# A float32 model step on one core: two projections go row tile by row tile, the weights' remainders last

## The chip, the cores and the metric

The kernel runs on one NeuronCore of one Trainium2 chip. The metric is the device time of one execution in microseconds (us). The engines are TensorE (PE), VectorE (DVE), ScalarE (ACT), GpSimd (POOL) and SyncE (SP), which issues most transfers.

## What is computed

For 256 rows (tokens) of width 1024 in float32, two blocks follow each other. The first: an FFT and convolution mixer, cross attention over a memory, and a mixture of 32 experts. The second, which the change touches, in the reference's words:

```
x = rmsnorm(x, norm_final)                         # end of the first block
for layer in range(2):
    shift, scale, gate = ada_modulation(c, ada_w[layer, 0], ada_b[layer, 0])
    h = x * (1.0 + scale) + shift
    y = mixer_ab(h, ...) or mixer_c(h, ...)        # layer 0: h @ ab_w_in (1024 x 1224); layer 1: h @ c_w_in (1024 x 3072)
    x = layer_norm(DN_ALPHA * x + gate * y, ln_g[layer, 0], ln_b[layer, 0])
    shift, scale, gate = ada_modulation(c, ada_w[layer, 1], ada_b[layer, 1])
    h = x * (1.0 + scale) + shift
    x = layer_norm(DN_ALPHA * x + gate * squared_relu_mlp(h, ...), ln_g[layer, 1], ln_b[layer, 1])
```

"Later projections" are those four inputs h of the second block, numbered m0 to m3: m0 goes into `ab_w_in`, m2 into `c_w_in`, m1 and m3 into the MLPs.

## The kernel before

Everything is written out by hand, engine by engine; each engine has one list of instructions, and semaphores tie the lists together. There is no planner: the order in the code is the order on the engine.

Most products are float32 made of three passes. Weights and inputs are split into a main part ("hi", rounded to fp32r) and a remainder ("lo" = value - hi), and `three` (L1192) adds x_hi w_hi, x_hi w_lo and x_lo w_hi into one bank. In the projections the piece of x is the stationary operand (128 x 128), the weights move (408 or 512 columns).

Weights come in granules of 2 MB or less through a ring of slots; SyncE issues a granule's transfer when the slot's former granule has been used up (semaphore `granules_used`, raised by the last matmul on it). ScalarE makes the main part (`split_hi`, L535), VectorE the remainder (`split_lo`, L545; `ab_in_lo`, L2285 to L2292, for the first granule of `ab_in`, in three pieces of 1224 columns). `ab_in` has granules of 3, 3 and 2 chunks of 128 rows; `c_in` six granules of 4 chunks, two for each of its three projections.

How x gets to TensorE: the row tiles (t = 0, 1; 128 rows each) are normalized in `X`; `transpose_hat` (L1697) transposes all 16 blocks of 128 x 128 into banks 4 to 7, a chunk k of both tiles side by side; ScalarE's `evac_hi` (L957, instruction at L967) writes scale * x + shift as main part into `XT_r`, 256 columns at a time, and VectorE's `evac_lo` (L2471, instructions at L2482 and L2487) the remainder into `XTL`. A chunk is usable when both are done (semaphores `xt_a`, `xt_v`).

- m0: behind the last expert, ScalarE splits granule 0 of `ab_in` (its last expert step is written out behind the loop for that), loads the table of the square root, splits granule 1, and squares the rows (L926) once VectorE has added the experts' sum (L2283). VectorE normalizes (L2298, L2299), TensorE transposes behind two filler matmuls (`keep_busy`, L1183), then runs 144 products chunk by chunk: for each chunk both tiles, for each tile three column groups, for each group three passes. At L1849 and after it follow small steps of the attention.
- m2: behind the first MLP, `layer_norm(1)` gives tile 0, then tile 1 (VectorE L2443 and ScalarE L954 write it). TensorE transposes tile 0, runs three filler matmuls, transposes tile 1, then runs `project3` on `c_in`: 96 products for each of the three projections. Between them VectorE makes the remainders of `c_in` 1 to 3, finishes the normalized rows (`affine`) and rotates the first projection's output (`rope`), which the third projection's banks wait for. The split of granules 0 and 1 has been done in the MLP (granule 0's remainder too).

## Time and profile before

| | |
|---|---|
| median of 3 runs | 1861.13 us (1860.92 to 1867.56) |
| profiled execution, its own time | 1863.54 us |
| its span | 1861.7 us |
| PE busy | 1761.7 us (95%) |
| DVE busy | 741.2 us (40%) |
| ACT busy | 533.8 us (29%) |
| share of the chain that ended last | PE 70%, DMA 21%, ACT 4%, DVE 3% |

The durations of the prediction are those of the profiled execution. In the rows, a line "start, length, engine, line, operation, out<-in, form, xN" groups N instructions; the length is that of the whole group, and "idle before <-releaser" tells how long the engine stood and what ended it. ACTq is ScalarE's queue, not its arithmetic. The profile counts a filler matmul (plain float32, 128 x 512) as two instructions.

### The profile page before, as it was taken

What the parts mean: (1) busy time and instruction counts of PE and PEld (TensorE: products, weight loads), DVE (VectorE), ACT (ScalarE), POOL (GpSimd) and SP (SyncE); (2) the same over time, 40 slices, a digit from 0 to 9 for tenths busy, and PEclk for the clock granted to TensorE, in tenths of its full rate; (3) what the DMA queues carried; (4) which work ended last, traced back from release to release, by engine and by line L of the source; (5) the groups of instructions that cost most, each with busy time, mean ns of one, the idle gap of its engine ahead of it and who ended that gap; (6) DMA issues with size and microseconds to landing.
All of it is one profiled execution on the core that took longest, in us unless ns stands there. A gap on an engine that the chain in (4) does not pass through costs nothing.

```text
span 1861.7 us, 24404 instructions
## 1 busy us (share of the span) xinstructions
PE 1761.7 (95%) x9962; PEld 1104.2 (59%) x9962; DVE 741.2 (40%) x1253; ACT 533.8 (29%) x693; POOL 28.2 (2%) x33
## 2 busy tenths in 40 slices
PE   6999999999999999999999999798899999989997
PEld 6787764344444343343434434375699878679986
DVE  3245352122222122121212212368865468675545
ACT  4344430110110110101101010327544453644442
POOL 0101000000000000000000000000000000000001
PEclk9999999999999999999999999998999999999999
DMA  9767899999999999999999999964345555435550
GB/s 340 284 222 279 295 391 428 427 428 427 428 429 429 428 428 428 428 428 429 429 429 428 428 428 429 372 214 169 116 172 189 196 189 187 175 114 181 180 203 24
DMA packets 96703, 587.68 MB, mean 316 GB/s; under 512 B 7118, under 2 KB 7332, under 8 KB 71044
## 3 DMA queue, kind: packets, MB, share of 16 engines
q1 hardware_dynamic: 95348, 582.12, 77.4%
q10 hardware_dynamic: 1296, 4.72, 0.7%
q8 instruction: 44, 0.72, 0.2%
q14 instruction: 15, 0.12, 0.0%
HBM read 585.77 MB, written 1.05 MB: 315 GB/s over the span
## 4 chain that ended last, share of the span: by engine, by line
PE 70%; DMA 21%; ACT 4%; DVE 3%; issue 1%; SPq 0%; ACTq 0%; DVEq 0%
PE bank L1192 34%; DMA ring<-in_w_gate_up 20%; PE bank L1486 14%; PE bank L1505 8%; PE bank L1433 4%; PE bank L1516 1%; PE bank L1281 1%; PE bank L1266 1%; PE bank L1478 1%; ACT arena L906 1%; PE bank L1498 1%; PE bank L1667 1%; ACT w_hi L535 1%; PE bank L1849 0%; PE bank L1654 0%
## 5 line engine op out<-in xcount | busy, mean ns | idle before, releaser
L1486 PE MATMUL bank<-ring,arena 128*64 128x512 f32 x2048 | 463.3, 597 | 31.4 <-DMA ring<-in_w_gate_up 31.4
L1486 PEld LDWEIGHTS bank<-ring,arena 128*64 128x64 f32 x2048 | 137.3, 136 | 323.5 <-issue 253.9
L1192 PE MATMUL bank<-w_hi,arena_r 128*128 128x512 f32 (+1 forms) x784 | 257.8, 391 | 4.7 <-DVE arena_r L2333 2.8
L1505 PE MATMUL bank<-ring,arena 128*64 128x512 f32 x1024 | 226.8, 595 | 3.3
L545 DVE TENSOR_TENSOR w_lo<-ring,w_hi 128x4096 fp32r<-128x4096 f32 (+2 forms) x43 | 188.1, 4375 | 53.0 <-ACT w_hi L535 50.8
L535 ACT ACTIVATE w_hi<-ring 128x4096 fp32r<-128x4096 f32 (+2 forms) x45 | 159.0, 3573 | 45.4 <-DMA ring<-in_c_w_out 25.4
L904 ACT ACTIVATE arena<-arena,sb_tab 128x512 f32<-128x512 f32 x32 | 23.1, 722 | 511.8 <-DVE arena L2188 511.8
L2188 DVE TENSOR_SCALAR arena<-bank 128x512 f32<-128x512 f32 x32 | 22.1, 692 | 370.7 <-PE bank L1486 370.7
L1192 PEld LDWEIGHTS bank<-w_hi,arena_r 128*128 128x128 f32 x784 | 148.1, 189 | 35.5 <-DVE arena_r L2333 3.3
L1505 PEld LDWEIGHTS bank<-ring,arena 128*64 128x64 f32 x1024 | 71.7, 137 | 137.8 <-issue 132.2
L1192 PE MATMUL bank<-XT_r,w_hi 128*128 128x256 f32 x512 | 146.5, 286 | 4.4 <-DVE arena_r L2487 4.4
L1192 PE MATMUL bank<-arena_r,w_hi 128*128 128x256 f32 x512 | 145.5, 284 | 0.0
L1192 PE MATMUL bank<-XT_r,w_lo 128*128 128x256 f32 x512 | 145.4, 284 | 0.0
L1433 PEld LDWEIGHTS bank<-arena,sb_XN 128*128 128x128 f32 x1056 | 123.2, 192 | 26.0 <-issue 26.0
L1433 PE MATMUL bank<-arena,sb_XN 128*128 128x64 f32 x1056 | 128.4, 275 | 0.0
L1192 PE MATMUL bank<-w_lo,arena_r 128*128 128x512 f32 x320 | 124.9, 390 | 0.0
L2209 DVE SCALAR_TENSOR_TENSOR arena_r<-bank,sb_att,arena_r 128x512 fp32r<-128x512 f32 x32 | 24.0, 750 | 217.4 <-ACT arena_r L909 217.4
L1192 PEld LDWEIGHTS bank<-XT_r,w_hi 128*128 128x128 f32 x512 | 98.9, 193 | 5.8 <-issue 5.3
L1192 PEld LDWEIGHTS bank<-arena_r,w_hi 128*128 128x128 f32 x512 | 98.9, 193 | 1.0 <-issue 0.5
L1192 PEld LDWEIGHTS bank<-XT_r,w_lo 128*128 128x128 f32 x512 | 98.8, 193 | 0.0
L909 ACT ACTIVATE arena_r<-bank,sb_att 128x512 fp32r<-128x512 f32 x32 | 22.0, 688 | 231.1 <-PE bank L1505 231.1
L522 DVE TENSOR_TENSOR half_lo<-ring,half_hi 128x2048 fp32r<-128x2048 f32 x24 | 55.0, 2291 | 81.2 <-ACT half_hi L512 81.1
(389 smaller groups left out, 2103.1 us busy)
## 6 DMA issues: line engine op xcount, KB each, us to landing
ring<-in_w_gate_up SPq DMA_DIRECT2D x128, 2048.0 KB, 32.0
ring<-in_w_down SPq DMA_DIRECT2D x64, 2048.0 KB, 35.3
ring<-in_mlp_w SPq DMA_DIRECT2D x32, 2048.0 KB, 8.3
ring<-in_ada_w SPq DMA_DIRECT2D x22, 2048.0 KB, 12.0
ring<-in_c_w_in SPq DMA_DIRECT2D x6, 2048.0 KB, 7.7
ring<-in_w_in SPq DMA_DIRECT2D x4, 2048.0 KB, 9.8
ring<-in_w_k SPq DMA_DIRECT2D x2, 2048.0 KB, 12.4
ring<-in_w_v SPq DMA_DIRECT2D x2, 2048.0 KB, 8.5
```

Source lines behind the costliest of these rows:

```text
L522: eng.tensor_tensor(lo[:], half_raw(name, h)[1], hi[:].bitcast(F32), ALU.subtract).then_inc(sem("w_lo"), 1)
L535: act.activation(pair(g)[0][:, 0:w], slot(slot_of(g), w), ACT.Copy).then_inc(sem("w_hi"), 1)
L545: eng.tensor_tensor(lo[:, 0:w], slot(slot_of(granule_no(name, i)), w), hi[:, 0:w].bitcast(F32), ALU.subtract).then_inc(sem("w_lo"), 1)
L904: act.activation(sig, gcl, ACT.Sigmoid, bias=zero, scale=1.702).then_inc(sem("e_sig"), 1)
L906: act.activation(hT, B[0][:].rearrange("p (c n) -> p c n", c=4), ACT.Copy).then_inc(sem("e_hTe"), 1)
L909: act.activation(y_hi, B[2][:], ACT.Copy, scale=slot_gate).then_inc(sem("e_y"), 1)
L1192: mm = pe.matmul(out, st[a], mv[b], start=start and a + b == 0, stop=stop and a == 1, skip_group_check=True)
L1433: mm = pe.matmul(B[3][:, k * CAP:(k + 1) * CAP], XN[:, t, k * P:(k + 1) * P], sel_tok[:, t, :], start=(t == 0), stop=(t == 1))
L1486: mm = pe.matmul(B[m][CAP * h:CAP * h + CAP, :], xe[:, 2 * j + kl, :], w[:, kl, m * D + h * HW:m * D + (h + 1) * HW], start=False, stop=(j ...
L1505: mm = pe.matmul(B[2][CAP * h:CAP * h + CAP, :], hT[:, c, CAP * j:CAP * j + CAP], w[:, c, h * HW:(h + 1) * HW], start=(j == 0 and c == 0), ...
L2188: dve.tensor_scalar(gcl, B[0][:], 7.0, None, ALU.min).then_inc(sem("e_clamp"), 1)
L2209: dve.scalar_tensor_tensor(y_lo, B[2][:], slot_gate, y_hi.bitcast(F32), ALU.mult, ALU.subtract).then_inc(sem("e_ylo"), 1)
```

## The change

1. ScalarE's last expert step goes back into the loop. The first two thirds of granule 0 of `ab_in` are split before the squares, the last third after the second root; granule 1 is split between the evacuations of the two tiles, no longer ahead of the squares.
2. VectorE makes the first two pieces of the remainder behind tile 0's and tile 1's normalization, the third behind the second.
3. For m0 and m2 the transposes go tile by tile: tile t uses banks 4 + 2t and 5 + 2t, 128 columns a block, and both engines evacuate 128 columns at a time (twice as many instructions of half the size). For m2 the first four blocks of tile 0 are evacuated before tile 1's root.
4. TensorE no longer runs `three` there but a written order of steps (granule, tile, x part, w part): main parts first, the weights' remainder last in each granule, and products of tile 0 ahead of the transposes of tile 1. Filler: five matmuls instead of two at m0, none instead of three at m2.

```diff
-            def expert(i, down_done, ahead=None):
+            def expert(i, down_done):
...
-                if ahead is not None:
-                    split_hi(act, *ahead)
-
-            with act.Fori(0, NE - 1) as i:
+
+            with act.Fori(0, NE) as i:
                 expert(i, (used, i * PER_E + (NPRE + PER_E)))
-            expert(NE - 1, (used, MOE_END), ("ab_in", 0))
...
             act.activation(stat[:, 59:60], eps5, ACT.Sqrt, bias=zero)
-            split_hi(act, "ab_in", 1)
+            ab_in_hi(0, 2)
...
+            def evac_tile(a, t, ks):
+
+                g1, g0 = modcol(a)
+                act.wait_ge(sem("mod_g"), 4)
+                for k in ks:
+                    if k % 4 == 0:
+                        act.wait_ge(*upto(f"m{a}", "T", 2 * t + k // 4 + 1))
+                    act.activation(XT_r[:, k, t * P:(t + 1) * P], B[4 + 2 * t + k // 4][:, k % 4 * P:k % 4 * P + P],
+                                   ACT.Identity, scale=g1(k), bias=g0(k)).then_inc(sem("xt_a"), 1)
...
-            evac_hi(0)
+            ab_in_hi(2, 3)
+            evac_tile(0, 0, range(KC))
+            split_hi(act, "ab_in", 1)
+            evac_tile(0, 1, range(KC))
             split_hi(act, "ab_in", 2)
...
             ln_hat(1, 0)
+            evac_tile(2, 0, range(4))
             ln_root(1, 1)
             ln_hat(1, 1)
-
-            evac_hi(2)
+            evac_tile(2, 0, range(4, KC))
+            evac_tile(2, 1, range(KC))
...
+            def project_tiles(a, grans, outs, width, order, ready):
+
+                for step in order:
+                    if step == "T":
+                        transpose_tile(a, 1)
+                        continue
+                    if step == "banks":
+                        pe.wait_ge(*upto(f"m{a}", "xt_v", KC))
+                        continue
+                    n, t, xa, wa, last = step
+                    parts, ks = grans[n]
+                    for kl, k in enumerate(ks):
+                        pe.wait_ge(*upto(f"m{a}", ("xt_a", "xt_v")[xa], KC * t + k + 1))
+                        ready(n, wa, kl)
+                        x = (XT_r, XTL[a])[xa]
+                        for c, b in enumerate(outs[t]):
+                            mm = pe.matmul(b, x[:, k, t * P:(t + 1) * P], parts[wa][:, kl, width * c:width * c + width],
+                                           start=k + xa + wa == 0, stop=False, skip_group_check=True)
+                    if last:
+                        mm.then_inc(used, 1)
...
-            keep_busy(0, 2)
-            transpose_hat(0)
...
+            keep_busy(0, 5)
+            transpose_tile(0, 0)
...
+                          [(0, 0, 0, 0, False), "T", (0, 0, 0, 1, False), (0, 0, 1, 0, False), (1, 0, 0, 0, False), "banks",
+                           (0, 1, 0, 0, False), (0, 1, 0, 1, False), (1, 1, 0, 0, False), (0, 1, 1, 0, True),
+                           (1, 0, 1, 0, False), (1, 1, 1, 0, False), (1, 0, 0, 1, False), (1, 1, 0, 1, True),
+                           (2, 0, 0, 0, False), (2, 1, 0, 0, False), (2, 0, 1, 0, False), (2, 1, 1, 0, False),
+                           (2, 0, 0, 1, False), (2, 1, 0, 1, True)], ab_in_ready)
...
-            transpose_hat(2)
+            transpose_tile(2, 0)
             x2 = (XT_r, XTL[2])
-            project3(x2, 0, ready=2)
...
+                          [(0, 0, 0, 0, False), (0, 0, 0, 1, False), "T", (0, 0, 1, 0, False), (0, 1, 0, 0, False),
+                           (0, 1, 0, 1, False), (1, 0, 0, 0, False), (1, 1, 0, 0, False), (0, 1, 1, 0, True),
+                           (1, 0, 1, 0, False), (1, 1, 1, 0, False), (1, 0, 0, 1, False), (1, 1, 0, 1, True)], c_in_ready)
...
-            ab_in_lo(0)
             for t in range(TB):
                 dve.wait_ge(*upto("fin", "root", t + 1))
                 link(dve.reciprocal(stat[:, 80 + t:81 + t], stat[:, 18 + t:19 + t]))
                 dve.tensor_scalar(X[:, t, :], X[:, t, :], stat[:, 80 + t:81 + t], None, ALU.mult).then_inc(
                     sem("xhat"), 1)
-            ab_in_lo(1)
+                ab_in_lo(dve, t)
+            ab_in_lo(dve, 2)
```

How the lists move, at the places of the prediction. TensorE at m0, behind the experts, before:

```order
L1183 MATMUL bank<-sb_tab 128x512 x2
L1710 MATMUL bank<-sb_tab,sb_X 128x128 [waits xhat]
L1710 MATMUL bank<-sb_tab,sb_X 128x128 x7
L1710 MATMUL bank<-sb_tab,sb_X 128x128 [waits xhat]
L1710 MATMUL bank<-sb_tab,sb_X 128x128 x7
L1192 MATMUL bank<-w_hi_49,XT_r 128x408 [waits xt_v,xt_a,ab_in_part]
L1192 MATMUL bank<-w_lo_50,XT_r 128x408
L1192 MATMUL bank<-w_hi_49,arena_r 128x408
```

and now (XT_r is x's main part, arena_r its remainder):

```order
L1217 MATMUL bank<-sb_tab 128x512 x5
L1763 MATMUL bank<-sb_tab,sb_X 128x128 [waits xhat]
L1763 MATMUL bank<-sb_tab,sb_X 128x128 x7
L1783 MATMUL bank<-w_hi_49,XT_r 128x408 [waits ab_in_hi,xt_a]
L1783 MATMUL bank<-w_hi_49,XT_r 128x408 x2
L1783 MATMUL bank<-w_hi_49,XT_r 128x408 [waits ab_in_hi,xt_a]
L1783 MATMUL bank<-w_hi_49,XT_r 128x408 x2
L1783 MATMUL bank<-w_hi_49,XT_r 128x408 [waits w_hi,xt_a]
L1783 MATMUL bank<-w_hi_49,XT_r 128x408 x2
L1763 MATMUL bank<-sb_tab,sb_X 128x128 [waits xhat]
L1763 MATMUL bank<-sb_tab,sb_X 128x128 x7
L1783 MATMUL bank<-w_lo_50,XT_r 128x408 [waits ab_in_part,xt_a]
```

Nine products of tile 0 have moved ahead of tile 1's transposes, and each run of three has its own two waits.

ScalarE at the same place, from the end of the experts on, now:

```order
L933 ACT_TABLE_LOAD
L933 ACTIVATE sb_stat<-sb_tab 128x1
L940 ACTIVATE w_hi_49<-ring 128x2448 [waits slot7_landed]
L946 ACTIVATE sb_XN,sb_stat<-sb_X,sb_tab 128x1024 [waits moe_x]
L949 ACTIVATE sb_stat<-sb_stat,sb_tab 128x1 [waits sq]
L946 ACTIVATE sb_XN,sb_stat<-sb_X,sb_tab 128x1024 [waits moe_x]
L949 ACTIVATE sb_stat<-sb_stat,sb_tab 128x1 [waits sq]
L940 ACTIVATE w_hi_49<-ring 128x1224 [waits slot7_landed]
L997 ACTIVATE XT_r<-bank,sb_mod 128x128 [waits T,mod_g]
```

Before the squares stand 2448 columns of split, where two splits of 3672 stood.

TensorE at m2, behind the first MLP, now (before: eight transposes, three fillers, eight transposes, then the products of `three`):

```order
L1763 MATMUL bank<-sb_tab,sb_X 128x128 [waits xhat_a]
L1763 MATMUL bank<-sb_tab,sb_X 128x128 x7
L1783 MATMUL bank<-w_hi_51,XT_r 128x512 [waits w_hi,xt_a]
L1783 MATMUL bank<-w_hi_51,XT_r 128x512
...
L1783 MATMUL bank<-w_lo_52,XT_r 128x512 [waits w_lo,xt_a]
L1783 MATMUL bank<-w_lo_52,XT_r 128x512
L1763 MATMUL bank<-sb_tab,sb_X 128x128 [waits xhat]
L1763 MATMUL bank<-sb_tab,sb_X 128x128 x3
L1763 MATMUL bank<-sb_tab,sb_X 128x128 [waits xhat_a]
L1763 MATMUL bank<-sb_tab,sb_X 128x128 x3
L1783 MATMUL bank<-w_hi_51,arena_r 128x512 [waits w_hi,xt_v]
```

Sixteen products of tile 0 stand where the fillers stood.

## Rows read from the trace of the kernel before

**Rows 1.** The page: granted clock in 40 slices, and the chain that ended last, by line.

```profile
PEclk9999999999999999999999999998999999999999
...
PE bank L1192 34%; DMA ring<-in_w_gate_up 20%; PE bank L1486 14%; PE bank L1505 8%; PE bank L1433 4%; PE bank L1516 1%; PE bank L1281 1%; PE bank L1266 1%; PE bank L1478 1%; ACT arena L906 1%; PE bank L1498 1%; PE bank L1667 1%; ACT w_hi L5
```

**Rows 2.** The chain in order of time, first place: start us, us, what.

```profile
1210.29 28.56 PE bank L1192 x144
1238.88 1.57 DVE arena L2545 x3
```

**Rows 3.** The same view, second place.

```profile
1534.47 56.30 PE bank L1192 x240
1590.79 7.64 DMA ring<-in_c_w_out
```

**Rows 4.** Windows: us, busy of each engine, PEclk (granted clock), DMA share, GB/s.

```profile
1204.00:1206.00 2.00, 0.67 (x3) 0.67 (x4) 1.10 (x4) 1.72 (x4) 0.00 (x0) 0.50 1.05 386
...
1535.00:1538.00 3.00, 3.00 (x8) 2.33 (x8) 2.93 (x9) 3.00 (x3) 0.00 (x0) 0.50 0.00 0
```

**Rows 5.** Timeline, ScalarE, first place: start us, us, engine line op, idle before.

```profile
1194.82 3.26 ACT L535 ACTIVATE w_hi<-ring 128x3672 fp32r<-128x3672 f32 x1
1198.09 1.28 ACT L922 ACT_TABLE_LOAD   x1
...
1199.59 3.25 ACT L535 ACTIVATE w_hi<-ring 128x3672 fp32r<-128x3672 f32 x1
1202.74 1.13 ACT L926 ACTIVATE sb_XN<-sb_X,sb_tab 128x1024 f32<-128x1024 f32 x1
...
1207.82 3.76 ACT L967 ACTIVATE XT_r<-bank,sb_mod 128x256 fp32r<-128x256 f32 x8 [2.07 <-PE bank L1710]
1211.43 2.28 ACT L535 ACTIVATE w_hi<-ring 128x2448 fp32r<-128x2448 f32 x1
```

**Rows 6.** The chain in order of time, ScalarE's queue (ACTq) in the first place.

```profile
1194.34 0.48 ACTq L917
...
1195.34 0.02 ACTq L531
```

**Rows 7.** Timeline, VectorE, first place.

```profile
1197.30 2.48 DVE L2283 TENSOR_TENSOR sb_X<-bank,sb_X 128x512 f32<-128x512 f32 x4 [1.59 <-PE bank L1516]
...
1206.65 1.43 DVE L2292 TENSOR_TENSOR w_lo<-ring,w_hi 128x1224 fp32r<-128x1224 f32 x1
```

**Rows 8.** Timeline, TensorE, first place; the last two are consecutive.

```profile
1205.33 3.67 PE L1710 MATMUL bank<-sb_tab,sb_X 128*128 128x128 f32 x16 [6.21 <-DVE sb_X L2299]
...
1217.59 0.35 PE L1192 MATMUL bank<-w_hi,XT_r 128*128 128x408 f32 x1
1217.77 0.34 PE L1192 MATMUL bank<-w_lo,XT_r 128*128 128x408 f32 x1
```

**Rows 9.** Timeline, TensorE, second place.

```profile
1527.61 1.03 PE L1710 MATMUL bank<-sb_tab,sb_X 128*128 128x128 f32 x8
1528.48 2.74 PE L1183 MATMUL bank<-sb_tab 128*128 128x512 f32 x6
1531.48 1.09 PE L1710 MATMUL bank<-sb_tab,sb_X 128*128 128x128 f32 x8 [0.26 <-DVE sb_X L2443]
...
1535.19 0.63 PE L1192 MATMUL bank<-w_hi,arena_r 128*128 128x512 f32 x1
1535.62 0.63 PE L1192 MATMUL bank<-w_hi,XT_r 128*128 128x512 f32 x1
```

**Rows 10.** Timeline, VectorE, second place.

```profile
1530.88 0.54 DVE L2443 TENSOR_SCALAR sb_X<-sb_X,sb_att 128x512 f32<-128x512 f32 x1
1533.06 0.88 DVE L2482 SCALAR_TENSOR_TENSOR sb_XN<-bank,sb_mod,XT_r 128x256 f32<-128x256 f32 x2 [1.64 <-ACT XT_r L967]
1533.97 0.62 DVE L2487 TENSOR_SCALAR arena_r<-sb_XN,sb_mod 128x256 fp32r<-128x256 f32 x2
...
1538.94 13.49 DVE L545 TENSOR_TENSOR w_lo<-ring,w_hi 128x4096 fp32r<-128x4096 f32 x3
```

More of the change, by code:

```diff
@@ L204 @@
     SHARES[_kind] = [(st, 4) for st in TURNS]
-SHARES["xt_a"] = [(st, 4 if st == "ffn" else 8) for st in TURNS]
+SHARES["xt_a"] = [(st, {"ffn": 4, "m0": 16, "m2": 16}.get(st, 8)) for st in TURNS]
 SHARES["xt_v"] = SHARES["xt_a"]
@@ L546, in split_lo, with ab_in_lo @@
                               ALU.subtract).then_inc(sem("w_lo"), 1)
+        def ab_in_lo(eng, k):
+            g = granule_no("ab_in", k // 3)
+            n, cut = split_no(g), slice(k % 3 * 1224, (k % 3 + 1) * 1224)
+            hi, lo = pair(g)
+            if k < 2:
+                eng.wait_ge(sem("ab_in_hi"), 1)
+            else:
+                eng.wait_ge(sem("w_hi"), n)
+            eng.wait_ge(sem("w_lo"), n - 1)
+            ins = eng.tensor_tensor(lo[:, cut], slot(slot_of(g))[:, cut], hi[:, cut].bitcast(F32), ALU.subtract)
+            ins.then_inc(*((sem("w_lo"), 1) if k % 3 == 2 else (sem("ab_in_part"), 1)))
         @block.sync
@@ L922, in _, with ab_in_hi @@
             act.activation(stat[:, 59:60], eps5, ACT.Sqrt, bias=zero)
-            split_hi(act, "ab_in", 1)
+            def ab_in_hi(a, b):
+                g = granule_no("ab_in", 0)
+                cut = slice(a * 1224, b * 1224)
+                act.wait_ge(landed[slot_of(g)], FILL[g])
+                act.activation(pair(g)[0][:, cut], slot(slot_of(g))[:, cut], ACT.Copy).then_inc(
+                    *((sem("w_hi"), 1) if b == 3 else (sem("ab_in_hi"), 1)))
+            ab_in_hi(0, 2)
             for t in range(TB):
@@ L1715, in transpose_hat, with transpose_tile @@
                         keep_busy(0, 3)
+            def transpose_tile(a, t):
+                st = "fin" if a == 0 else f"ln{a - 1}"
+                if a == 0:
+                    pe.wait_ge(*upto(st, "xhat", t + 1))
+                elif t == 0:
+                    pe.wait_ge(*upto(st, "xhat_a", 1))
+                else:
+                    pe.wait_ge(*upto(st, "xhat", 1))
+                for k in range(KC):
+                    if a and t == 1 and k == 4:
+                        pe.wait_ge(*upto(st, "xhat_a", 2))
+                    mm = pe.transpose(B[4 + 2 * t + k // 4][:, k % 4 * P:k % 4 * P + P], X[:, t, k * P:(k + 1) * P], ident)
+                    if k % 4 == 3:
+                        mm.then_inc(sem("T"), 1)
+            def project_tiles(a, grans, outs, width, order, ready):
[17 more added lines that the diff above has]
+                        mm.then_inc(used, 1)
             def x_chunk(a, k):
@@ L1915, in _, with c_in_ready @@
             mlp(0)
-            transpose_hat(2)
+            transpose_tile(2, 0)
             x2 = (XT_r, XTL[2])
-            project3(x2, 0, ready=2)
+            g2 = at[0]
+            at[0] += 2
+            def c_in_ready(n, wa, kl):
+                pe.wait_ge(sem(("w_hi", "w_lo")[wa]), split_no(g2 + n))
+            project_tiles(2, [(chunks(pair(g2 + j), 4), range(4 * j, 4 * j + 4)) for j in range(2)],
+                          [[B[2 * t + h][:] for h in range(2)] for t in range(TB)], HW,
+                          [(0, 0, 0, 0, False), (0, 0, 0, 1, False), "T", (0, 0, 1, 0, False), (0, 1, 0, 0, False),
+                           (0, 1, 0, 1, False), (1, 0, 0, 0, False), (1, 1, 0, 0, False), (0, 1, 1, 0, True),
+                           (1, 0, 1, 0, False), (1, 1, 1, 0, False), (1, 0, 0, 1, False), (1, 1, 0, 1, True)], c_in_ready)
             project3(x2, 4)
@@ L2469, in affine_ready, with evac_tile @@
                     dve.wait_ge(*upto(f"ln{a - 1}", "ln_landed", 32))
+            def evac_tile(a, t):
+                g1, g0 = modcol(a)
+                for q in range(2):
+                    dve.wait_ge(*upto(f"m{a}", "xt_a", KC * t + 4 * q + 4))
+                    for k in range(4 * q, 4 * q + 4):
+                        if t:
+                            dve.wait_ge(*upto(f"m{a}", "xt_v", k + 1))
+                        ins = dve.scalar_tensor_tensor(XN[:, 0, k * P:(k + 1) * P], B[4 + 2 * t + q][:, k % 4 * P:k % 4 * P + P],
+                                                       g1(k), XT_r[:, k, t * P:(t + 1) * P].bitcast(F32), ALU.mult,
+                                                       ALU.subtract)
+                    link(ins)
+                    for k in range(4 * q, 4 * q + 4):
+                        dve.tensor_scalar(XTL[a][:, k, t * P:(t + 1) * P], XN[:, 0, k * P:(k + 1) * P], g0(k), None,
+                                          ALU.add).then_inc(sem("xt_v"), 1)
             def evac_lo(a):
@@ L2474, in evac_lo @@
                 for q in range(4):
-                    if a == 0 and q == 1:
-                        ab_in_lo(2)
                     dve.wait_ge(*upto(f"m{a}", "xt_a", 2 * q + 2))
@@ L2520, in mlp @@
                 mlp_group(l, 3, True, ahead)
-            evac_lo(0)
+            for t in range(TB):
+                evac_tile(0, t)
             split_lo(dve, "ab_in", 1)
@@ L2627, in _ @@
             layer_norm(1, "mlp0", 15)
-            evac_lo(2)
+            for t in range(TB):
+                evac_tile(2, t)
             for i in range(1, 4):
```

40 lines of the change are left out of this document (10 added, 30 removed).

## The prediction

> **What bounds the kernel now.** I read four views in this order. First the chain that ended last, by line [rows 1]: TensorE's matmuls of the split products (L1192) hold 34% of the span and the experts' weights most of the rest, so TensorE is the bound outside the expert loop. Then the same chain in order of time around the two places that the change touches. In the first place (after the last expert) 144 matmuls of `ab_in` run from 1210.29 for 28.56 us, and at 1238.88 the copies of the result start [rows 2]; the transposes ahead of them start at 1205.33 [rows 8]. In the second place (behind the first MLP) 240 matmuls of `c_in` start at 1534.47, and a transfer follows them [rows 3]. All of what stands ahead of 1210.29 and 1534.47 is exposed. Third the windows: the granted clock is 0.50 (the 1.2 GHz level) in 1204 to 1206 and again in 1535 to 1538 [rows 4], behind 6.21 us and 1.9 us in which TensorE stood idle [rows 8, 9]. Last the timelines of the three engines in the two places [rows 5 to 10], for durations.
>
> **The change, stage one.** ScalarE today splits a whole granule after its last expert step (3.26 us), loads a table (1.28), splits a second granule (3.25), and squares the first rows only at 1202.74 [rows 5]. The change leaves two thirds of one split there. ScalarE's queue got past the skipped overflow block at 1195.34 [rows 6], so I put the table load at 1195.5; plus 1.28, plus 0.2 for the one-element root (what lies between the table load and the split at 1199.59), plus 2.28 (the row of 2448 columns) gives the square at 1199.3, 3.4 us sooner. VectorE's adds of both row tiles start at 1197.30 and take 2.48 for four [rows 7], so the first tile is there. Everything that hangs on the square moves by 3.4: the transposes from 1205.33 to 1201.9.
>
> The Trainium skill's page "Runtime: NRT & Kernel Launch", section "Instruction fetch mechanics", speaks against this move: a taken branch that leaves the prefetched pages must first fetch its target. The same skip in the trace cost no more than 1.0 us from the read of the count (1194.34) to the next wait (1195.34) [rows 6], then hidden behind the 3.26 us split. By the trace the stage gains what is worked out here; by the rule it would begin later by one fetch, which no row prices, and this is part of rival two.
>
> TensorE's filler grows from 2 to 5 matmuls. The profile counts each as two; six of these took 2.74 us [rows 9], with the tail about 0.43 each, so ten end near 1201.6, ahead of the transposes. TensorE is then idle for some 1.3 us in pieces, not the 6.21 us of before [rows 8], and I take the clock to stay at 2.4 GHz.
>
> ScalarE next makes the last third (1.1), from 1202.3 to 1203.4, then eight 128-column evacuations. Eight of 256 columns took 3.76 [rows 5]; the slope between the two split rows (3.25 and 2.28 us for 3672 and 2448 columns) is 0.8 ns a column, so one of 128 costs about 0.36. That is 16 x 0.36 = 5.8 in place of 3.8 us, beside TensorE's work. The first product starts at 1203.9. A product costs 0.185 us at full clock [rows 8]. Nine (1.7) reach 1205.6, the second tile's transposes (its rows ready at 1204.2) 1206.5. The nine with the weights' remainder need VectorE: norm of tile 0 ends 1201.9, a third of the remainder 1.43 [rows 7] 1203.3, norm of tile 1 1204.2, two more thirds 1207.0. So these end at 1208.2. The nine with x's remainder need VectorE's first small pieces. From the 256-column pairs (0.88 and 0.62 for two [rows 10]; the second duration is that of the same operation in the first stage) less 128 elements I take 0.3 and 0.2; four and one, with the link between, reach 1208.6. **This is the one wait I expect.** From there 144 - 18 = 126 products x 0.185 = 23.3 end at 1231.9. Against 1238.7 (1210.29 + 28.56, less about 0.15 for the tail of the last record) that is **-6.8 us**.
>
> Later needs, with their slack: granule 1 main part 1209.5 (needed 1210.2); banks of tile 0 read by VectorE 1211.2 (needed 1211.9); remainder of granule 1 1219.3, that is four quarters of 2.0 us and at most three thirds of 1.43 [rows 7] behind 1207.0 (needed 1221.9); of granule 2 about 1224.6 (needed 1229.7). The bounds of the 128-column pieces, which today's kernel does not have: if halving saves nothing (VectorE 0.44 and 0.31, ScalarE 0.47), the bank wait costs 1.1 us, the remainder of granule 1 another 0.3, and in stage two the remainder of c_in 2 comes 1.2 us late; if it halves the cost, only the wait at 1208 goes (0.4). I take the values by the slope, which are nearest to the rows, and keep +2.6 and -0.4 for the range.
>
> **Stage two.** Today the transposes of tile 0 start at 1527.61, three filler matmuls follow, tile 1's transposes take 1.09 from 1531.48 after a wait of 0.26 [rows 9], and the first product waits 1.9 us more, with the first nine at 0.43 in place of 0.227 us ((56.30 - 9 x 0.43) / 231 = 0.227 [rows 3, 9]). The change fills the gap: evacuation of four chunks of tile 0 from 1528.2, sixteen products of granule c_in 0 (main part and remainder were made in the MLP) from 1528.7. 16 x 0.227 = 3.6 gives 1532.3; I take 1532.0, since the last product's tail overlaps what follows. The transposes' inputs are there by then: VectorE's part by 1531.42 [rows 10], and the same transposes ran through from 1531.48 [rows 9]. They reach 1533.0. x's remainder for tile 0: VectorE free at 1531.4, first chunk at about 1532.9. Then 80 x 0.227 = 18.2 end at 1551.2. Before: 1534.47 + 9 x 0.43 + 87 x 0.227 = 1558.1. That is **-6.9 us**; if the sixteen really end at 1532.3, -6.6.
>
> What is late next: VectorE's evacuation takes 4 x 2.0 = 8.0 in place of 5.9 us but starts at 1531.4, not 1533.06; its three weight remainders (13.49 [rows 10]) then start near 1539.3, and hand over at 1543.8, 1548.3 and 1552.8, needed at 1547.5, 1551.2 and 1562. After them come two affine steps and the rotations of the first 1024 columns, ready near 1566, needed by the third projection at 1573. The output projection's second granule is fetched when c_in 4 is used up, a TensorE event, so the 7.64 us transfer in the chain [rows 3] moves with it. Removing the three filler matmuls is free: the products stand in their place.
>
> Granules go back to the fill queue later in the order (the first after 72 products, not 54, and after 64, not 48) but not later in time: 1218.5 where it is about 1222 today, and 1543.9 where it is about 1547, so SyncE's queue, which waits for nothing else there, sends each transfer sooner.
>
> The same holds between the stages: no transfer ends a wait in the chain from 1210 to 1590 but that one, so stage one's gain arrives at the end. The peeled last expert step going back into ScalarE's loop costs nothing by itself; it only removes code.
>
> **Sum.** -6.8 - 6.9 = -13.7 us, of which about 0.4 us is in doubt by the sixteen. The profiled execution (span 1861.7, itself 1863.54) becomes 1849.8; the median of the three runs, 1861.13, becomes 1847.4. I say 1847.5. A measurement of this kernel tells about 0.5%, or 9.3 us, from no change: faster means under 1851.8.
>
> **Rivals.** *One, the clock sinks anyway.* For: in both places an idle stretch was followed by 0.50 [rows 4], and some idle pieces stay in stage one. Against: they are 1.3 us together, and stage two has almost none. Price: nine products at 0.43 in place of 0.227 cost 1.8 us; once or twice gives 1849.3 to 1851.1, still faster. The page "TensorE: Matmul & The Clock Gate", section "HAM oscillation — how this bites in real kernels", says that work behind a long enough wait starts cold. By that rule, which the rows around 1204 bear out, fewer waits keep it warm.
>
> *Two, only one stage pays.* Stage one rests on ScalarE starting at once after a loop exit, a load and a branch, and on two slacks of 0.7 us; stage two on VectorE's queue. If either stage gives nothing, -6.8: 1854.3, within 0.5%. Against: no row shows such a delay.
>
> *Three, slower.* Products now take x and weights in runs of three (stage one) or two (stage two), and each run has two waits of its own: 144/3 + 96/2 = 96 pairs, where it was one pair per 18 or 12. If every pair stopped TensorE as a wait that really ends late does (0.26 us idle before the transposes at 1531.48 [rows 9]), 96 x 0.26 = 25.0 us would turn -13.7 into +11.3: 1872.4. It breaks even at 0.14 us a pair. Against: in `c_in` today two waits per twelve products show no gap within 56.30 us [rows 3], so a wait that is already met costs nothing at that density. At 0.05 to 0.14 us a pair this is part of the "no change" case.
>
> **Numbers.** Forecast 0.67; clock 0.13; one stage or half-paid waits 0.16; slower 0.04. Faster: 0.67 + 0.13 = 0.80; same 0.16; slower 0.04. The range reaches down to 1844, since the span has one more slice whose mean clock is 8 tenths [rows 1], and a low stretch there may shorten when the work behind stage one comes sooner (3 us, an estimate from that digit), and up to 1855, past the one-stage case.
>
> **What would show it.** The profile after should have the transposes near 1202, `ab_in` done by 1232, one short wait for VectorE at 1208, clock 1.00 through 1202 to 1214 and (6.8 earlier than today's times) through 1525 to 1531, and `c_in`'s first projection over 13.7 us sooner. Wrong would be: 128-column evacuations over 0.45 us, gaps between runs of three products, a table load on ScalarE later than 1196, or VectorE's remainder of granule 1 after TensorE wants it.

## The result, and the profile after

The changed kernel takes **1850.97 us** (median of 6 executions, 1844.03 to 1851.34), the kernel before 1862.63 (median of 6). The ratio is 0.9924, 95% interval [0.9904, 0.9944]. The profiled execution took 1850.79 us with a span of 1849.0, where the one before had 1861.7: -12.7 us.

The page of the changed kernel, busy line and the slices of the granted clock:

```profile
PE 1759.2 (95%) x9962; PEld 1103.7 (60%) x9962; DVE 744.7 (40%) x1285; ACT 539.0 (29%) x711; POOL 28.1 (2%) x33
...
PEclk9999999999999999999999999998999999999999
```

The clock's line is digit for digit that of [rows 1]. Its slices of 46 us are too coarse for what follows: low stretches have moved between the two kernels, and only windows show it.

**Stage one.** The chain in order of time (start us, us, what):

```profile
1201.44 1.94 PE bank L1783 x9
1203.38 0.87 PE bank L1763 x8
1204.25 25.13 PE bank L1783 x135
1229.38 0.02 issue
1229.41 1.57 DVE arena L2627 x3
```

The copies of the result start at 1229.41 where they started at 1238.88 [rows 2], 9.47 us sooner. But not all of this is the change's. The timeline of TensorE of the kernel before has the last product of the expert loop at

```profile
1195.85 1.19 PE L1516 MATMUL bank<-arena_r 64*128 64x512 f32 x8 [1.73 <-DVE arena_r L2209]
```

and that of the changed kernel, from the same product on,

```profile
1193.82 1.19 PE L1550 MATMUL bank<-arena_r 64*128 64x512 f32 x8 [1.67 <-DVE arena_r L2286]
1195.14 4.56 PE L1217 MATMUL bank<-sb_tab 128*128 128x512 f32 x10
1199.53 1.07 PE L1763 MATMUL bank<-sb_tab,sb_X 128*128 128x128 f32 x8
1201.44 1.94 PE L1783 MATMUL bank<-w_hi,XT_r 128*128 128x408 f32 x9 [0.84 <-ACT XT_r L997]
1203.22 1.03 PE L1763 MATMUL bank<-sb_tab,sb_X 128*128 128x128 f32 x8
1204.01 1.90 PE L1783 MATMUL bank<-w_lo,XT_r 128*128 128x408 f32 x9
1205.76 1.93 PE L1783 MATMUL bank<-w_hi,arena_r 128*128 128x408 f32 x9
```

The expert loop, which the change leaves to the weights' transfers, ended 2.03 us sooner in this execution. From that product to the copies it is 43.03 us before and 35.59 after: **-7.44 us**. The first product starts 7.62 us behind the expert product (1201.44), where it started 14.44 us behind it (1210.29 [rows 2]). The idle time ahead of it explains most of that: 0.84 us now, in place of 6.21 us ahead of the transposes [rows 8] and 1.29 us more behind them. The remainder products at 1205.76 have no idle time in brackets: the wait for VectorE that I expected there is absent.

The engines that feed them, ScalarE and then VectorE, timelines:

```profile
1193.29 1.28 ACT L933 ACT_TABLE_LOAD   x1 [0.40 <-issue]
1194.58 0.29 ACT L933 ACTIVATE sb_stat<-sb_tab 128x1 f32<-128x1 f32 x1
1194.78 2.23 ACT L940 ACTIVATE w_hi<-ring 128x2448 fp32r<-128x2448 f32 x1
1196.92 1.13 ACT L946 ACTIVATE sb_XN<-sb_X,sb_tab 128x1024 f32<-128x1024 f32 x1
...
1200.95 2.87 ACT L997 ACTIVATE XT_r<-bank,sb_mod 128x128 fp32r<-128x128 f32 x8
```

```profile
1204.26 1.12 DVE L2546 SCALAR_TENSOR_TENSOR sb_XN<-bank,sb_mod,XT_r 128x128 f32<-128x128 f32 x4
1205.42 0.88 DVE L2551 TENSOR_SCALAR arena_r<-sb_XN,sb_mod 128x128 fp32r<-128x128 f32 x4
```

The square starts 3.10 us behind the expert product (6.89 before, [rows 5]). Eight pieces of 128 columns take ScalarE 2.87 us, 0.36 each; four take VectorE 1.12 and 0.88. A quarter (four and four) takes 1.95 us, from 1204.26 to the next at 1206.21.

**Stage two.** The chain, then rows of TensorE's timeline:

```profile
1522.58 3.96 PE bank L1783 x16
1526.53 0.87 PE bank L1763 x8
1527.41 18.16 PE bank L1783 x80
```

```profile
1521.37 1.03 PE L1763 MATMUL bank<-sb_tab,sb_X 128*128 128x128 f32 x8
1522.58 2.13 PE L1783 MATMUL bank<-w_hi,XT_r 128*128 128x512 f32 x8 [0.17 <-ACT XT_r L997]
...
1545.41 0.39 PE L1226 MATMUL bank<-w_hi,XT_r 128*128 128x512 f32 x1
```

The transposes of tile 0 start at 1521.37 (1527.61 before, [rows 9]); sixteen products fill the gap, and the next projection starts at 1545.41. That is 24.04 us behind the transposes. Before, it was 30.35 us (the 97th of the 240 products of [rows 3] starts at 1557.96): -6.3 us.

**The clock, and what went back.** Windows of the changed kernel (columns: us, busy of PE, PEld, DVE, ACT, POOL, then the granted clock as a share of 2.4 GHz, DMA share, GB/s):

```profile
1194.00:1232.00 38.00, 37.03 (x206) 31.45 (x209) 29.70 (x64) 21.96 (x38) 0.00 (x0) 1.00 0.64 232
1238.00:1242.00 4.00, 4.00 (x6) 1.50 (x5) 3.27 (x16) 0.00 (x0) 0.00 (x0) 0.58 1.06 389
1262.00:1273.00 11.00, 9.31 (x38) 5.41 (x38) 10.31 (x41) 10.50 (x25) 0.00 (x0) 0.53 0.00 1
1283.00:1290.00 7.00, 7.00 (x36) 3.37 (x35) 4.29 (x17) 3.05 (x11) 0.00 (x0) 0.51 0.12 23
1337.00:1341.00 4.00, 3.53 (x17) 3.56 (x18) 3.92 (x12) 1.50 (x4) 0.00 (x0) 0.57 0.14 57
1516.00:1550.00 34.00, 33.83 (x158) 27.95 (x157) 32.16 (x55) 19.11 (x23) 0.00 (x0) 1.00 0.45 158
```

Both stages run at 1.00 throughout; in both the kernel before had 0.50 windows [rows 4]. So part of both gains is the clock. In stage two the kernel before had nine products at 0.43 in place of 0.227 us, 1.8 us. In stage one its products stood 0.34 us apart at first, in place of 0.185:

```profile
1211.11 0.54 PE L1192 MATMUL bank<-w_hi,arena_r 128*128 128x408 f32 x1
1211.45 0.54 PE L1192 MATMUL bank<-w_hi,XT_r 128*128 128x408 f32 x1
```

The low stretch ended at 1213.9, some ten products in, which makes about 1.6 us, an estimate from these two distances; its transposes were slow too.

Between the stages TensorE sits at 1.2 GHz for 23.8 us, summed over windows of 1 us, and the kernel before only for 17.0 (23.9 and 17.1 by the clock's own records). The way from the copies of stage one to the transposes of stage two grew from 288.73 to 291.96 us: 3.2 us of stage one's gain went back there. The experiments had to tell whether the change does that.

I cut each execution at five marks: E, the expert product above; Z, the copies; M, the first product behind the first attention; T, the transposes of stage two; Y, the first product behind the second attention. In brackets: us at 1.2 GHz in the stretch (behind Y the low stretch at the program's end, which every kernel has, is left out).

| kernel | E to Z | Z to M | M to T | T to Y | Y to end |
|---|---|---|---|---|---|
| before | 43.03 (10.2) | 74.96 (17.0) | 213.77 (0) | 109.82 (3.4) | 224.27 (3.4) |
| changed | 35.59 (0) | 76.71 (20.4) | 215.25 (3.4) | 103.38 (0) | 224.25 (3.4) |
| changed, again | 35.60 (0) | 73.06 (13.6) | 213.77 (0) | 103.52 (0) | 224.38 (3.4) |
| s1_only | 35.60 (0) | 75.03 (17.0) | 215.26 (3.4) | 109.78 (3.4) | 224.41 (3.4) |
| s2_only | 43.07 (10.2) | 74.98 (17.0) | 213.79 (0) | 104.81 (3.4) | 224.43 (3.4) |
| t_first | 35.71 (0) | 76.56 (20.4) | 215.29 (3.4) | 108.94 (6.8) | 224.51 (3.4) |
| fill2 | 36.16 (3.4) | 71.63 (10.2) | 215.15 (3.4) | 104.80 (3.4) | 224.49 (3.4) |
| split_back | 40.49 (3.4) | 73.09 (13.6) | 213.74 (0) | 103.63 (0) | 224.32 (3.4) |
| lo_early | 38.90 (3.4) | 71.55 (10.2) | 215.07 (3.4) | 106.25 (3.4) | 224.27 (3.4) |
| warm_mlp | 35.58 (0) | 73.36 (13.6) | 213.75 (0) | 103.43 (0) | 223.01 (0) |
| warm_mlp, again | 35.60 (0) | 73.57 (13.6) | 213.75 (0) | 104.88 (3.4) | 222.98 (0) |
| warm_ix | 35.57 (0) | 77.15 (13.6) | 215.08 (3.4) | 104.84 (3.4) | 224.44 (3.4) |
| warm_all | 37.06 (3.4) | 79.40 (20.4) | 213.74 (0) | 106.60 (6.8) | 222.96 (0) |

### The profile page after: what moved, and what is told of

Same layout as the page of the kernel before. It is cut to its first block, busy times and chain, and to the rows that moved or that the text cites. A ratio compares the mean times of both kernels' runs of the same rounds, so it can differ in the third digit from the quotient of the medians.

```text
span 1849.0 us, 24540 instructions
## 1 busy us (share of the span) xinstructions
PE 1759.2 (95%) x9962; PEld 1103.7 (60%) x9962; DVE 744.7 (40%) x1285; ACT 539.0 (29%) x711; POOL 28.1 (2%) x33
## 4 chain that ended last, share of the span: by engine, by line
PE 73%; DMA 20%; ACT 4%; DVE 3%; issue 1%; SPq 0%; ACTq 0%; DVEq 0%
PE bank L1226 32%; DMA ring<-in_w_gate_up 19%; PE bank L1520 15%; PE bank L1539 8%; PE bank L1467 4%; PE bank L1783 3%; PE bank L1550 1%; PE bank L1315 1%; PE bank L1300 1%; PE bank L1512 1%; ACT arena L920 1%; PE bank L1532 1%; PE bank L1701 1%; PE bank L1688 0%; PE bank L1916 0%
## 5 line engine op out<-in xcount | busy, mean ns | idle before, releaser
L1226 PE MATMUL bank<-w_hi,arena_r 128*128 128x512 f32 x704 | 227.5, 392 | 4.7 <-DVE arena_r L2400 2.8
L1226 PEld LDWEIGHTS bank<-w_hi,arena_r 128*128 128x128 f32 x704 | 132.3, 188 | 33.9 <-DVE arena_r L2400 3.3
```

The lines of the kernel that those rows point to most:

```text
L1226: mm = pe.matmul(out, st[a], mv[b], start=start and a + b == 0, stop=stop and a == 1, skip_group_check=True)
```

## The experiments

**One stage each.** s1_only keeps the first stage and restores the third projection; s2_only the reverse.

```diff
-            transpose_tile(2, 0)
...
+            transpose_hat(2)
+            x2 = (XT_r, XTL[2])
+            project3(x2, 0, ready=2)
```

> The first stage as changed, the third projection as it was before. My theory: the stages gain by themselves, and what lies between gives some back by the granted clock. The first stage's consumers should come 7.4 us sooner than before (and the two or so more that the expert loop may take less by itself), the way from the second attention's transposes to the first output 63.9 us as before (1527.6 to 1591), and the whole 1854 to 1858 us. Rival, only one stage pays and it is the second: 1861 to 1863. Rival, the clock's low stretches move with every shift of a few us: then the sum is off from 1862.6 - 7.4 - 2 by one or two times 1.7 us, and the windows show another count of low stretches between the stages.

> The third projection as changed, the first stage as it was. My theory: the stretches up to 1527 us of the span read as before, the way from the first transposes of that stage to the first output load shrinks by 6.3 us, and the whole is 1855.5 to 1857 us; the low stretches of the clock ahead of the stage lie where they lay before (1248, 1272 to 1282, 1292, 1535 us). Rival, only the first stage pays: 1862 to 1863. Where the two single runs together take off 3 us more than the changed kernel did, the 3 us are given back only when the two shifts meet.

s1_only: 1856.85 us (median of 10), ratio 0.9964 [0.995, 0.9978]. s2_only: 1856.73 (10), 0.9978 [0.9962, 0.9995]. By the table the stages' gains are independent: 35.60 and 109.78 us in the one, 43.07 and 104.81 in the other. Rival two, that only one stage pays, is out for the first stage as for the second. Both medians lie in the ranges that I expected. Against the kernel before in the same series (1862.76) they are 5.9 and 6.0 us lower, 11.9 together, and the changed kernel was 11.7 lower in its own series, so the totals show no loss that comes only when both changes meet. My expectation for s2_only erred in its detail: a new low stretch at 1625 cost 1.4 us, and its executions spread from 1854.4 to 1863.84.

**The transposes first.** Tile 1's transposes ahead of all products, in both places.

```diff
-                          [(0, 0, 0, 0, False), "T", (0, 0, 0, 1, False), (0, 0, 1, 0, False), (1, 0, 0, 0, False), "banks",
+                          ["T", (0, 0, 0, 0, False), (0, 0, 0, 1, False), (0, 0, 1, 0, False), (1, 0, 0, 0, False), "banks",
...
-                          [(0, 0, 0, 0, False), (0, 0, 0, 1, False), "T", (0, 0, 1, 0, False), (0, 1, 0, 0, False),
+                          ["T", (0, 0, 0, 0, False), (0, 0, 0, 1, False), (0, 0, 1, 0, False), (0, 1, 0, 0, False),
```

> The changed kernel with tile 1's transposes ahead of every product in both places. My theory: in the first stage nothing of weight (tile 1's rows are there before tile 0's first evacuated piece, so the transposes fill that wait): 0 to +0.4 us; in the third projection TensorE stands until the second tile's normalised rows come and the sixteen products of tile 0 no longer lie in that wait: +3.6 to +4.0 us; together 1854.5 to 1855.5 us. Rival, the products in that wait only displace products that would have waited for VectorE's evacuation anyway: 0 to +1 us, 1851 to 1852. Second rival: the idle engine lets the clock sink, +1.8 us more, up to 1857.

1856.62 us (7), 0.9963 [0.9951, 0.9974], above the 1854.5 to 1855.5 of my theory and within the second rival's reach. Stage one 35.71: +0.1. Stage two, TensorE's timeline:

```profile
1522.05 1.03 PE L1763 MATMUL bank<-sb_tab,sb_X 128*128 128x128 f32 x8
1525.92 1.97 PE L1763 MATMUL bank<-sb_tab,sb_X 128*128 128x128 f32 x8 [2.83 <-DVE sb_X L2510]
1527.54 2.87 PE L1783 MATMUL bank<-w_hi,XT_r 128*128 128x512 f32 x8
```

2.83 us idle, then transposes that take 1.97 in place of 1.03 and eight products 2.87 in place of 2.13: the clock has sunk. From the transposes to the next projection it is 28.17 us (1550.22) against 24.04: +4.1. About 1.7 us of this are the clock (0.94 in the transposes, 0.74 in the products); the rest is the idle time that the sixteen products had filled. So these products are worth 4.1 of stage two's 6.3 us, partly because they keep the engine at work and the clock up, and next to nothing of stage one's gain comes from the products ahead of the second transposes.

**The place of the squares.** split_back puts granule 0's last third and granule 1's split back ahead of the squares.

```diff
             ab_in_hi(0, 2)
+            ab_in_hi(2, 3)
+            split_hi(act, "ab_in", 1)
             for t in range(TB):
...
-            ab_in_hi(2, 3)
             evac_tile(0, 0, range(KC))
-            split_hi(act, "ab_in", 1)
```

> The changed kernel with the third piece of granule 0 and all of granule 1 split by ScalarE ahead of the squares again (the split of granule 1 was there before the change). My theory: the first product of the stage hangs on the squares, so it comes later by these two instructions, 1.1 + 3.2 = 4.3 us, and nothing behind takes it back, because TensorE works without a wait from its first product on: from the last expert's product to the copies of the projection's result 35.6 us become 39.5 to 40.0, and 1 us more where the idle engine's clock falls: 1855 to 1856.5 us. Rival, the order of the products made the gain and the squares' place did not: 35.6 to 37 us, 1851 to 1852.5.

TensorE then reads

```profile
1201.78 1.09 PE L1763 MATMUL bank<-sb_tab,sb_X 128*128 128x128 f32 x8 [4.08 <-DVE sb_X L2365]
1203.05 3.36 PE L1783 MATMUL bank<-w_hi,XT_r 128*128 128x408 f32 x9 [0.17 <-ACT XT_r L999]
```

The stage takes 40.49 us, +4.9. The transposes start 4.24 us later behind the expert product (9.95 against 5.71 us), as two instructions more in the queue should give. The first product starts 3.60 us later (11.22 against 7.62), because granule 0's last third no longer stands between transposes and evacuation. The nine products then take 3.36 us, not 1.94: 1.4 us for the clock, which fell behind 4.08 us idle. All but 0.1 reaches the copies. **Putting this order of ScalarE's queue back costs 4.9 us, two thirds of stage one's 7.4: 3.6 by the wait, the rest by the clock that the wait let fall.** The other third is not taken apart to the end: the half-size evacuations were not tested alone. The whole took 1850.94 us (median of 4, 1848.93 to 1856.71), ratio 0.9951 [0.9934, 0.9967], not the 1855 to 1856.5 that I expected. The changed kernel in the same series had 0.9939 [0.992, 0.9958], so the totals do not show the 4.9 us. The profiled execution had no low stretch between M and Y, as the changed kernel's second had none. The spread over so few executions (8 and 13 us) is larger than the effect; only the marks, of one profile, resolve it.

**The weights' remainder products early.** lo_early puts them right behind the main ones of their granule and tile:

```diff
...
-                           (0, 1, 0, 0, False), (0, 1, 0, 1, False), (1, 1, 0, 0, False), (0, 1, 1, 0, True),
-                           (1, 0, 1, 0, False), (1, 1, 1, 0, False), (1, 0, 0, 1, False), (1, 1, 0, 1, True),
+                           (0, 1, 0, 0, False), (0, 1, 0, 1, False), (0, 1, 1, 0, True),
+                           (1, 0, 0, 0, False), (1, 0, 0, 1, False), (1, 0, 1, 0, False),
...
```

> The changed kernel with the weights' remainder products right behind the main ones of their granule and tile in both places instead of last; tiles stay apart. My theory: in the first stage granule 1's remainder, which VectorE finished at about 1216.3 us of the span, is wanted by TensorE at about 1214, so 2 to 2.5 us of waiting come in: from the last expert's product to the copies of the projection's result 35.6 us become 37.6 to 38.1; in the third projection the remainders are there in time and the stage keeps its length (103.4 us, or 104.8 with a low stretch of the clock near 1620); the whole 1852 to 1854 us plus or minus the clock. Rival, putting these products last buys nothing: 35.6 us stay.

```profile
1193.25 6.25 PE L1217 MATMUL bank<-sb_tab 128*128 128x512 f32 x10
...
1215.57 1.91 PE L1783 MATMUL bank<-w_lo,XT_r 128*128 128x408 f32 x9 [2.09 <-DVE w_lo L545]
...
1533.57 2.08 PE L1783 MATMUL bank<-w_lo,XT_r 128*128 128x512 f32 x8 [0.99 <-DVE w_lo L545]
```

2.09 us of waiting, as expected, so "last" is worth 2 us in stage one. I missed two things. One is a wait of 0.99 in stage two, where T to Y takes 106.25, 1.4 more than 104.85 with the same low stretch. The other is the clock: five fillers took 6.25 us at the low level and held up the transposes, so that the first product came 1.0 us later (8.59 against 7.62), which brings stage one to +3.3. 1853.43 us (6), 0.9957 [0.9943, 0.997].

**The fillers of stage one.** fill2: two fillers instead of five (`keep_busy(0, 2)`).

> The changed kernel with two filler rounds instead of five ahead of the first stage's transposes. My theory, rival one of the prediction: TensorE then stands for about 2.7 us before the transposes, the granted clock may go to its lower level there, and one low stretch of 3.4 us at half rate costs 1.7 us, which shows as a window below 0.8 within 1199 to 1210: 1852.6 us. Other outcome: the gap is too short to matter, the clock stays at 1.00, 1850.8 to 1851.2 us, and the fillers that are needed were two. Nothing of the output depends on the fillers.

```profile
1196.15 1.98 PE L1217 MATMUL bank<-sb_tab 128*128 128x512 f32 x4
1200.56 1.97 PE L1763 MATMUL bank<-sb_tab,sb_X 128*128 128x128 f32 x8 [2.42 <-DVE sb_X L2365]
1202.49 2.61 PE L1783 MATMUL bank<-w_hi,XT_r 128*128 128x408 f32 x9
```

The clock fell, behind 2.42 us idle, but stage one lost 0.6 us, not 1.7. The slow transposes only used up the 0.84 us that TensorE stood before: the first product starts 7.62 us behind the expert product here too (1202.49), and only the nine products (2.61 in place of 1.94) add time. The whole was 1849.75 us (4), ratio 0.9936 [0.9914, 0.9958], lower than the 1850.97 of the changed kernel; in the profiled execution only 10.2 us were slow between Z and M. That says nothing for the two fillers. A total of these kernels also depends on how much low clock an execution happens to have.

**Fillers elsewhere.** warm_ix fills the 2.85 us idle in which the low stretch at 1262 begins; warm_mlp fills the 2.17 us ahead of the MLPs' first products; warm_all is both with fill2.

```diff
+            pe.wait_ge(sem("ix_relu"), 5)
+            keep_busy(6, 3)
             pe.wait_ge(sem("ix_relu"), 8)
...
                             pe.wait_ge(*upto(st, "xhat_a", 2))
+                        if a and t == 1 and k == 6:
+                            keep_busy(0, 2)
```

> The changed kernel with three rounds of filler matmuls in the 2.85 us in which TensorE stands before the third pair of scores of the first attention (1260.8 to 1263.7 us); nothing of the output depends on them. My theory: the six profiles so far have from the copies of the first projection's result to the transposes of the third projection 279.9 us plus half of the time that the granted clock was at its lower level (10.2 to 23.8 us of it), so the idle times there are paid through the clock. If this gap causes the 10.2 us low stretch at 1262.5, the way falls from 292.0 us to about 286.9; if the stretch only moves behind the next gaps, to 288.5 to 290.5; rival, the low stretch comes from something else: 292.0, or more by what the fillers delay. The whole 1845.8 us, 1848 to 1849, or 1851.

> The changed kernel with two rounds of filler matmuls inside the second tile's transposes of the two other projections (the hidden layers' inputs), where TensorE stands 2.17 us ahead of its first product; nothing of the output depends on them. My theory: the low stretches at 1337 and 1655 us of the changed kernel's profile (3.4 us each) go: 1.7 us less for each, 1847.5 us in all; at worst they delay the last evacuated piece by 0.2 us a place. Rival, the low stretches there come from the sparse work before, and stay: 1851.0 to 1851.4.

> The two kinds of filler together, and two rounds instead of five ahead of the first stage (0.6 us longer there in its profile, by a low stretch at 1200). My theory: the gains add as far as the low stretches go: 1843 to 1846 us. Rival, the low stretches only wander with any shift, so that this is one more throw between 1846 and 1854 us.

warm_ix: 1853.14 us (8), 0.9952 [0.9937, 0.9967], no gain. In the kernels without this filler Z to M follows one line: 71.6, 73.1 to 73.6, 75.0, 76.6 us for 10.2, 13.6, 17.0, 20.4 us slow. warm_ix has 13.6 and takes 77.15. Its timeline of TensorE:

```profile
1267.27 1.92 PE L1701 MATMUL bank<-ring,sb_cs 128*32 128x512 f32 x16
1272.19 0.87 PE L1688 MATMUL bank<-sb_tab,sb_XN 128*128 128x128 f32 x6 [3.00 <-DVE sb_XN L2452]
```

The stretch went from 1262, and TensorE then stood 3.00 us for VectorE's top-k and softmax. The six products at 1272.19 start 41.70 us behind Z, against 42.50 and 42.23 in the changed kernel's two profiles: the slow stretch taken away gave back 0.8 us at most. So the slow time there had mostly been hidden by VectorE; the new low stretch, at 1273 to 1281, lies where TensorE bounds. The line was a property of one pattern, and my theory that any filled gap pays is wrong. warm_all (1850.51 us, 5 executions, 0.9939 [0.9922, 0.9956]) missed its 1843 to 1846 us and shows the same: 79.40.

warm_mlp: 1846.46 us (4), 0.9912 [0.9889, 0.9936]; windows at its two places, to be read against 0.57 at 1337 above:

```profile
1337.00:1341.00 4.00, 3.55 (x24) 2.75 (x23) 3.81 (x11) 2.79 (x7) 0.00 (x0) 1.00 0.51 207
...
1655.00:1659.00 4.00, 3.52 (x29) 3.56 (x30) 3.92 (x12) 1.43 (x4) 0.00 (x0) 1.00 0.13 51
```

**Side by side.** The changed kernel and warm_mlp again, on one chip:

> The changed kernel as it is, for a comparison on one chip. Both theories: 1850 to 1852 us, the stage 35.6 us, the third projection's way 103.4 us or 104.8.

> The changed kernel with two filler rounds inside the second tile's transposes of the two hidden layers' inputs, again, beside the changed kernel. My theory: 2.5 to 4 us below it in the median (two low stretches of the clock at 1.3 to 1.7 us each), 1847 to 1848.5 us, with the first products of both places at 0.12 us a pair from the start. Rival, the 4.5 us between the medians so far were the luck of four runs: 1850 to 1852 us.

1849.02 us (6 executions, 1844.38 to 1856.94; ratio 0.9939 [0.992, 0.9958]) against 1848.09 (6, 1843.23 to 1851.22; 0.992 [0.9906, 0.9934]). The difference of 0.9 us is not the 2.5 to 4 that I expected, and the intervals overlap, so the total doesn't prove the fillers. The table does more: Y to end is 223.0 in all three kernels with them and 224.25 to 224.51 in the ten without, and M to T has no low stretch in three of three, where it had one in six of ten. That is -1.4 us in the second place, and -1.4 in the first whenever the clock would have sunk. Over all executions of both series, which ran on different chips, the medians are 1850.8 (12) and 1848.1 (10), 2.7 apart. It has the lowest median of all versions that I ran.

The changed kernel's second profile bears on the 3.2 us. Same program, other execution:

```profile
1261.00:1272.00 11.00, 8.41 (x35) 4.69 (x36) 10.23 (x39) 10.18 (x23) 0.00 (x0) 0.53 0.00 1
1283.00:1290.00 7.00, 6.90 (x63) 4.12 (x62) 6.49 (x29) 5.56 (x22) 0.34 (x2) 1.00 0.54 177
1333.00:1337.00 4.00, 3.12 (x26) 3.15 (x27) 3.89 (x13) 1.92 (x5) 0.00 (x0) 1.00 0.26 104
```

No low stretch at 1283 and none at the first MLP. Z to T takes 286.83 us, less than before the change, and the span is 1844.2. So the change does not have to give anything back. Whether it makes the give-back more likely is not shown. The two profiles with the old stage one have 288.73 and 288.77 us from Z to T; the nine with the new one and without filler between Z and M have 286.6 to 287.3 six times and 290.3 to 292.0 three times.

## Why the prediction was right, and where its steps were off

The total, 1847.5, was 3.5 us low; the range and the side were right (the ratio's interval ends at 0.9944, below the 0.995 that I had asked for). Of the 3.5 us, 1.5 are the starting point: I took the 1861.13 us of three executions, and the median of six is 1862.63. The other 2.0 are the gain, 11.7 us between the medians for the forecast 13.7. By its steps:

- **ScalarE ahead of the squares, -3.4**: right in kind, 0.4 short. Behind the expert product the square came 3.8 us sooner (6.89 to 3.10). The table load behind the loop's exit and the skipped block was there 0.2 us sooner than I put it, with 0.40 us idle ahead of it. The Trainium skill's page "Runtime: NRT & Kernel Launch" (section "Instruction fetch mechanics") says that a taken branch out of the prefetched pages must fetch its target first; the trace shows no wait longer than these 0.40 us. split_back gives the step from the other side: 3.6 us at the first product and 4.9 with the clock.
- **128-column pieces, 0.36 on ScalarE, 2.0 us a quarter on VectorE**: right (0.36; 1.95). The slope between two sizes of the same operation was a better guide here than halving or not halving.
- **"This is the one wait I expect", 0.4 us at 1208**: wrong, no wait. Counted from the expert product the first product came 0.4 us sooner than I had it, and VectorE's first pieces were there at 1205.7, where TensorE came for them at 1205.76. It cost the sum nothing, since the 126 products behind took 23.65 us, not 23.3.
- **Stage one, -6.8**: measured -7.44, three times over (35.59, 35.60, 35.60). Of the 0.6 missing, 0.4 is that earlier first product, the rest my reading of the old end as 1238.7, where [rows 2] has 1238.88. The absent wait (0.4) and the slower 126 products (0.35) cancel. With 1.6 us or more of low clock in the old stage, this step names the queue but not how much of its gain is the clock.
- **Stage two, -6.9, or -6.6 if the sixteen end late**: they did. In the chain they take 3.96 us, not the 3.6 by which even the late value went; the first eight, which follow ScalarE's pieces, need 1.96 us from start to start, not 1.82. To the next projection it gave -6.3, and T to Y -6.44 in the profile and -6.3 in the second. So this term was 0.3 to 0.6 us too large.
- **"No transfer ends a wait between the stages, so stage one's gain arrives at the end"**: true of transfers, but the step left out the clock. There are 13 to 24 us at 1.2 GHz between the stages in every profile, and the changed kernel's two differ by 10.2 us. In the first the way between them took 3.2 us back; in the second it took nothing. This is the step that failed: `c_in`'s second projection starts 12.55 us sooner (1545.41 against 1557.96) where over 13.7 was forecast, and that with the 2.03 us of the expert loop. The profile's account is -7.44 - 6.44 + 3.23 - 2.03 (expert loop) = -12.68, for -12.7 measured. The two stages together gave 13.9 us, a little more than the sum of the forecast; that this execution's total came near (12.7 for 13.7) is luck in part, the 2.0 us of the expert loop, which no step of the forecast moved. Behind the expert product the program is 10.7 us shorter in the first profile and 15.6 in the second. I had let the clock vary only by a slice at the front.
- **Rivals.** Rival one, the clock sinking anyway, did not come in the two stages of the changed kernel, but did elsewhere at about its price (1.4 us each, for 1.8). It came inside stage one in four of the variants (split_back, lo_early, fill2, warm_all). The rule of the Trainium skill's page "TensorE: Matmul & The Clock Gate" (section "HAM oscillation — how this bites in real kernels") that work behind a long wait starts cold agrees in kind with t_first, fill2 and split_back (2.4 to 4.1 us idle, then slow). It does not tell the cases apart that lie closer. In lo_early the clock fell during the fillers, behind 1.67 us idle ahead of the expert product, and stayed up in the changed kernel behind the same 1.67 us. The changed kernel's two profiles, with two idle pieces between 1277 and 1283 (0.80 and 1.70 us, then 0.51; 1.30 and 1.20 us, then 1.00), show that pieces of this size may or may not be followed by the low clock. Rival two fell with the single-stage runs. Rival three, a price for each met wait, fell too: 135 products with their pairs of waits run in 25.13 us, 0.186 each, the distance from product to product of before (0.185).

## What to carry to other kernels

Where one engine bounds, look not at its busy share but at the first instruction that it waits for, and clear the feeder's queue ahead of it: moving 4.3 us of splits behind ScalarE's squares was worth 4.9 us (3.6 of wait, the rest of clock), more than any order of the products that I tried. Put products whose operands are ready into a wait that already exists, and those whose operands come latest, last: here worth 4.1 us (1.7 of it clock) and 2.1 us. When effects are smaller than the spread of the totals (13 us here), cut the trace at fixed marks. The changed first stage then took 35.57 to 35.60 us in six profiles, and the changed third projection 103.38 to 103.63 in four, or 1.4 more where a low stretch of the clock fell into it; the stretch between them (Z to M) still varied by 5 us.

## What I had not expected of the hardware

- The granted clock's low stretches came as 3.4, 6.8 or 10.2 us in every profile, all but the one at the program's end (6.7 to 9.4 us). One of 3.4 us cost 1.4 to 1.7 us where TensorE bounds, down to 0.6 in stage one, and most of a 10.2 us stretch cost nothing where VectorE did (0.8 us at most came back when it was gone).
- Two executions of one program differed by 5.1 us in a stretch of 290 us, with 10.2 us less at the low clock. The mean granted clock went with the total: 0.993 for the changed kernel's 1844.03 and 1844.38 us, 0.985 for its 1856.94. What makes the clock sink in one and not in the other stays open.
- Fillers are matmuls too: at the low clock five of them took 6.25 in place of 4.56 us, and the first product behind them came 1.0 us later.
- The expert loop's end moved between 1191.8 and 1198.5 us over the thirteen profiles, whatever had been changed behind it. An end time is therefore no measure of a stage without a mark ahead of it.
